# Wider products in a causal convolution and in LayerNorm's sums of a hybrid encoder trunk

## The reference, cut to what matters

```python
def conv_module(h, buf, w_pw1, b_pw1, w_dw, b_dw, ln_g, ln_b, w_pw2, b_pw2):
    u = h @ w_pw1 + b_pw1
    a, gt = jnp.split(u, 2, axis=-1)
    glu = a * jax.nn.sigmoid(gt)
    xp = jnp.concatenate([buf.astype(glu.dtype), glu], axis=1)
    y = causal_dwconv(xp, w_dw, b_dw)          # 31 taps, each channel by itself
    y = jax.nn.silu(layernorm(y, ln_g, ln_b))  # mean and variance over the 1024 channels
    return y @ w_pw2 + b_pw2, new_buf
...
def rmsnorm(x, g):
    y = xf * lax.rsqrt(jnp.mean(xf * xf, axis=-1, keepdims=True) + EPS)
```

## Time and profile before

| | us |
|---|---|
| median of 3 runs | 2890.53 (2886.12 to 2891.44) |
| profiled execution | 2888.88 |
| its span, first to last instruction | 2887.1 |
| mean granted clock of TensorE, as a share of full speed | 0.986 |

### The profile page before, as it was taken

How to read it: one execution, slowest core, us unless ns; L and a number is a source line. 1 busy time by engine, 2 the same in 40 slices (tenths; PEclk the granted TensorE clock), 3 DMA queues, 4 the chain that set the end, 5 groups by cost and what they waited for, 6 DMA issues and landing times.

```text
span 2887.1 us, 40334 instructions
## 1 busy us (share of the span) xinstructions
PE 2849.4 (99%) x16832; PEld 2798.9 (97%) x16832; DVE 1662.5 (58%) x1821; ACT 529.3 (18%) x647; POOL 834.4 (29%) x686
## 2 busy tenths in 40 slices
PE   8999999999999999999999999999999999999998
PEld 8999799999999999999999999989999999999998
DVE  8995336454545455466676667781744555454445
ACT  3001323111111111231111111121311111111122
POOL 5221154222222222243121222114322222222224
PEclk9999599999999999999999999999999999999999
DMA  5223021111111111121111110103111111111112
GB/s 152 57 59 57 0 109 44 38 43 44 44 38 41 44 44 40 41 108 52 46 45 38 45 46 31 47 30 116 38 43 44 44 39 41 44 44 39 41 45 79
DMA packets 109012, 147.07 MB, mean 51 GB/s; under 512 B 65265, under 2 KB 78065, under 8 KB 108913
## 3 DMA queue, kind: packets, MB, share of 16 engines
q1 hardware_dynamic: 48624, 112.48, 12.3%
q10 hardware_dynamic: 60288, 33.14, 4.0%
HBM read 129.13 MB, written 16.47 MB: 50 GB/s over the span
## 4 chain that ended last, share of the span: by engine, by line
PE 89%; DVE 9%; issue 1%; ACT 1%; POOL 0%; DMA 0%; DVEq 0%; ACTq 0%; POOLq 0%
PE BANKS L649 63%; PE BANKS L895 11%; PE BANKS L937 3%; PE BANKS L1123 3%; DVE BANKS L1678 1%; PE BANKS L722 1%; PE BANKS L720 1%; PE BANKS L857 1%; DVE HGA L2032 1%; DVE HGA L1997 1%; DVE HGA L2019 1%; PE BANKS L745 1%; DVE XL L1590 1%; PE BANKS L986 1%; DVE X L1678 1%
## 5 line engine op out<-in xcount | busy, mean ns | idle before, releaser
L535 POOL TENSOR_TENSOR SMALL<-WRAW 128x1 f32<-128x1 f32 x196 | 48.4, 247 | 1916.3 <-PE BANKS L649 1334.1
L649 PE MATMUL BANKS<-XH,WH 128*128 128x384 f32 x2592 | 592.0, 336 | 0.6 <-DVE X L1603 0.5
L649 PE MATMUL BANKS<-XL,WH 128*128 128x384 f32 x2592 | 588.6, 334 | 0.0
L649 PE MATMUL BANKS<-XH,WL 128*128 128x384 f32 x2592 | 588.6, 334 | 0.0
L538 POOL TENSOR_TENSOR WL<-WRAW,WH 128x1024 fp32r<-128x1024 f32 x196 | 476.5, 2431 | 15.7
L649 PEld LDWEIGHTS BANKS<-XL,WH 128*128 128x128 f32 x2592 | 462.2, 188 | 0.0
L649 PEld LDWEIGHTS BANKS<-XH,WL 128*128 128x128 f32 x2592 | 462.1, 188 | 0.0
L649 PEld LDWEIGHTS BANKS<-XH,WH 128*128 128x128 f32 x2592 | 460.4, 188 | 1.7 <-DVE X L1603 0.9
L1815 DVE TENSOR_TENSOR X<-BANKS,X 128x1152 f32<-128x1152 f32 x168 | 228.0, 1357 | 267.4 <-PE BANKS L649 206.4
L1872 DVE SCALAR_TENSOR_TENSOR ARENA<-ARENA 128x1168 f32<-128x1168 f32 x176 | 255.7, 1453 | 130.9 <-ACT ARENA L1377 122.2
L1377 ACT ACTIVATE ARENA<-ARENA 128x1168 f32<-128x1168 f32 x88 | 120.3, 1367 | 943.7 <-DVE ARENA L1612 943.7
(11 more groups left out here) (214 smaller groups left out, 3474.7 us busy)
## 6 DMA issues: line engine op xcount, KB each, us to landing
WRAW<-in_w SPq DMA_DIRECT2D x188, 512.0 KB, 3.5
X<-in_x SPq DMA_DIRECT2D x8, 576.0 KB, 9.0
X<-in_x ACTq DMA_DIRECT2D x8, 576.0 KB, 7.2
x_kept<-X ACTq DMA_DIRECT2D x8, 576.0 KB, 2.8
X<-x_kept ACTq DMA_DIRECT2D x8, 576.0 KB, 7.4
HGA<-taps_padded ACTq DMA_DIRECT2D x32, 128.0 KB, 3.5
HGA<-in_state ACTq DMA_DIRECT2D x8, 512.0 KB, 4.3
out_hgs<-HGA ACTq DMA_DIRECT2D x8, 512.0 KB, 2.6
```

The source lines that it names most:

```text
L535: nc.gpsimd.tensor_tensor(PAD, one, one, ALU.mult)
L649: ins = nc.tensor.matmul(ps_bank(n, c), w, x[:, third(c)], start=(k == 0 and q == 0), stop=(k == last and q == 2), skip_group_check=betwee ...
```

## The change

- `convolved`: each product takes the same 40 columns three times over (120 columns, by a dimension of stride 0), and twice or once where the bank ends (the eleventh and the twelfth group of a full bank). The extra results fall where the next groups write later, each with `start=True`.
- Twelve products of `mean` instead of seven stand ahead of the convolution of c = 7, and nine among its groups.
- `variance` and `fin_sum` multiply with 128 columns of ones in place of one. ScalarE reads every 128th column of the result.
- `idle_products` are added, 256 columns each, two records each: six and two around the last three `mean` products, and two, one and three around `spread_norm(1)` and `spread_norm(2)`. TensorE's wait for a free slot stands ahead of the first of the latter.
- GpSimd's splits of the first two weight units of the next product wait until VectorE has transposed the last channel's data.

```diff
+            pool.wait_ge(xt_rdy, len(TOEPLITZ))
             split(U_PW2)
             split(U_PW2 + 1)
...
-                    out = PS[:, n % 2 * NCH + g // BANK_GROUPS, at:at + COLS]
-                    nc.tensor.matmul(out, WT[:, g, 0, :], XT[0][:, :, g], start=True, stop=False,
-                                     skip_group_check=True)
-                    ins = nc.tensor.matmul(out, WT[:, g, 1, :], XT[1][:, :, g], start=False, stop=True,
-                                           skip_group_check=True)
+                    times = min(3, (512 - at) // COLS)
+                    out = PS[:, n % 2 * NCH + g // BANK_GROUPS, at:at + times * COLS].rearrange(
+                        "p (r b) -> p r b", r=times)
+                    for t in range(2):
+                        blocks_of = XT[t][:, :, g].rearrange("p (r b) -> p r b", r=1).broadcast_to([P, times, COLS])
+                        ins = nc.tensor.matmul(out, WT[:, g, t, :], blocks_of, start=t == 0, stop=t == 1,
+                                               skip_group_check=True)
...
-            ahead = len(parts) - (BLK // 2 - 2)
+            ahead = 12
...
+            def idle_products(times, out):
+                for _ in range(times):
+                    nc.tensor.matmul(out[:, 0:2 * P], IDENT, CONST[:, 0:2 * P], start=True, stop=True)
+            idle_products(6, MB[:, 0, :])
             for c in range(NCH):
                 mean(KD - 1, c)
+            idle_products(2, MB[:, 0, :])
...
-                        ins = nc.tensor.matmul(ps_bank(T_VAR, c)[:, t:t + 1],
-                                               LSQ[:, KD * c + 2 * p, t * P:(t + 1) * P], ONES[:, 0:1],
+                        ins = nc.tensor.matmul(ps_bank(T_VAR, c)[:, t * P:(t + 1) * P],
+                                               LSQ[:, KD * c + 2 * p, t * P:(t + 1) * P], ONES,
...
             variance(2)
+            free_slot(T_PW2)
+            idle_products(2, ps_bank(T_PW2, 2))
             spread_norm(1)
+            idle_products(1, ps_bank(T_PW2, 2))
             spread_norm(2)
+            idle_products(3, ps_bank(T_PW2, 2))
             pe.wait_ge(w_split, U_PW2 + 2)
-            free_slot(T_PW2)
...
-                        ins = nc.tensor.matmul(MB[:, c % 2, t:t + 1], squares[:, a:a + P], ONES[:, 0:1],
+                        ins = nc.tensor.matmul(MB[:, c % 2, t * P:(t + 1) * P], squares[:, a:a + P], ONES,
```

More of the change, by code:

```diff
@@ L1333, in ln_root @@
                 act.wait_ge(var_full, c + 1)
-                A(R9[:, c * NCH:(c + 1) * NCH], ps_bank(T_VAR, c)[:, 0:NCH], ACT.Sqrt, bias=EPSC, scale=1.0 / D
+                A(R9[:, c * NCH:(c + 1) * NCH], ps_bank(T_VAR, c)[:, 0:CW:P], ACT.Sqrt, bias=EPSC, scale=1.0 / D
                   ).then_inc(root_rdy, 1)
@@ L1552, in _ @@
                 act.wait_ge(fin_sums, c + 1)
-                A(R9[:, c * NCH:(c + 1) * NCH], MB[:, c % 2, 0:NCH], ACT.Sqrt, bias=EPSC, scale=1.0 / D
+                A(R9[:, c * NCH:(c + 1) * NCH], MB[:, c % 2, 0:CW:P], ACT.Sqrt, bias=EPSC, scale=1.0 / D
                   ).then_inc(fin_root, 1)
```

## The result

The changed kernel's median is 2915.31 us (2915.23 to 2916.34, 4 runs) against 2890.8 for the kernel before. The ratio is 1.0087, with a 95% interval of 1.0071 to 1.0103. The forecast was 2902.5, slower, with 2861 to 2914 as its range: the sign was right, the forecast change of 12.0 us was half of the measured one, and the time lies 1.3 us above the range. The profiled execution took 2915.35 us, 26.5 more than that of before.

A forecast was written before the change was run, and what follows sets the result against it. The prediction took PE's own work as the bound: busy 99% of the span, 89% of the chain. Its terms summed to +12.0 us on the profiled 2888.88, so 2900.9, median 2902.5, range 2861 to 2914.

The forecast's parts named there:

- 1, 2: four channels, and the fall of the clock at 250 us: Channels between value tiles: 120-column records at 0.180 us add 30.7 us; no clock fall at 250 us saves 1.5.
- 3: the last channel: The last channel's mean products and convolution: 35.6 us at full clock in place of 50.65, so -15.1 us.
- 4: later splits: GpSimd's splits of the next weight units, moved behind VectorE's transposes: needed 60 us later, so 0.
- 5: six idle products: Six idle products after the last convolution: 2.6 us of work in a 2.6 us wait, +0.2 us (0 to +1).
- 6: mean product to centring: First mean product to VectorE's start: 0.81 us at full clock in place of 1.69, so -0.9 us.
- 7: spreading to the dense products: From `spread_norm(0)` to the first dense product: faster sums, three idle products give back 1.3 us; -1.0 us (-1.9 to +3).
- 8: the tail: `fin_sum(2)` and the spreading behind it, at about half clock before: -0.4 us (-1 to 0).
- The upper bound: A 120-column convolution record takes at most 0.200 us, by the half clock's rate of 1.65 ns per column.
- The rival of free columns: Convolution records of 120 columns keep 0.112 us: sum -26.3 us, median 2864; chance 0.36.
- The rival in between: Convolution records of 120 columns take 0.145 to 0.160 us: sum -8 to 0, median 2882 to 2891; chance 0.08.
- The falling clock: Clock falls despite width, slowing dense products and mean records: +19 to +25 us, median 2909 to 2916; 0.11 with late idle products.

The follow-up runs named there:

- pair120: The changed kernel with `XT` in pairs, the columns of two neighbouring groups alternating: 2861.23 us, ratio 0.9886 to the kernel before.
- trial of distances: The changed kernel with extra unread products at its end: 120 columns took 0.112 us a record two elements apart, 0.156 at three, 0.212 at four, 0.208 at 32.
- cols40: The changed kernel with the convolution's 40 columns taken once, all its other edits kept: 2866.25 us (2863.11 to 2874.88, 6 runs).
- pair120_sums1: pair120 with one column in both LayerNorm's and the last norm's sums, as before the change: 2865.82 us.

## Why the prediction was right in sign and wrong in size

Point by point, by the steps of the prediction:

| step | forecast us | measured us |
|---|---|---|
| 1, 2: four channels, and the fall of the clock at 250 us | +30.7 - 1.5 | +40.8 |
| 3: the last channel | -15.1 | -12.0 |
| 4: later splits | 0 | 0.0 (taken out of pair120) |
| 5: six idle products | +0.2 | 0.0 |
| 6: mean product to centring | -0.9 | -0.7 |
| 7: spreading to the dense products | -1.0 | -1.3 |
| 8: the tail | -0.4 | -0.3 |
| sum | +12.0 | +26.5 |

The step that failed is one number: "So I take 1.5 ns per column: 120 columns take 0.180 us". The price is 0.207, and 80 columns take two thirds of it, about 0.138 (four of them start within 0.4 us). Four channels then cost 4 x (112 x 0.095 + 8 x 0.026) = 43.4 us, 12.7 more than forecast; 1.1 more than forecast came back. Of these 0.6 can be TensorE's waits (0.63 us of 198 before, none after); the rest isn't traced. The last channel came out 3.1 above its forecast. 12.7 - 1.1 + 3.1 = 14.7 of the 14.5 us missed; the rest are tenths in steps 5 to 8.

The mechanism, a limit on the rate of reads, was read rightly off the 228 ns of the earlier trace rows, and the trial of distances bears it out; what was misread is the slope. I divided the whole excess over one column, 59 ns, by the 39 further columns. The least durations for 40, 80 and 120 columns are 228 ns, 299 and 365 ns: the first 40 cost 59, the next 40 cost 71, the last 40 cost 66. It is as if a few columns came for nothing at the start of a record and the rest cost 1.7 ns each. In a stream every column has that price, 0.207 us / 120 = 1.72 ns. The upper bound failed the same way: it was set at the half clock's 1.65 ns because there the excess seemed gone. But a read price of 1.72 ns beside the array's own 1.65 would make only 3 ns over 39 columns, too little to see, and no run shows that the price of reads is the same at both clocks. So that row could not bound the price at full clock. With 0.207 us for 120 columns and 0.138 for 80 the sum had been +28.

The rival of free columns had 0.36 and is out for this layout; its sum, 2864, is within 3 us of pair120, where its condition holds (2861.23). The rival in between, 0.145 to 0.160 us because reads run ahead while the weights load, is out by the same 0.207. The falling clock did not come: the clock stayed full among the last channel's groups, at 0.207 us a record. Term 7 had its disturbance, the clock fell for part of it (0.81 over the stretch), and still came out 0.3 us better than taken. What it had wrong is the price of the three idle products, 1.3 us: taken out of pair120 they change nothing, since they stand where TensorE waits for VectorE.

## What to carry to other kernels

Look at how far apart the columns of a moving operand lie before widening it: in these runs, at full clock, float32 columns up to 8 bytes apart cost no more than side by side and from 16 bytes on twice as much (1.72 ns against 0.83), and products of 40 columns hid that, since their records start 0.112 us apart either way. When a cost is hidden, take its slope from two sizes where it shows, not from one size and zero. And a layout with pairs may serve both the engine that writes and the one that reads, as it did here. Before paying for a higher clock, look for a wait ahead of the stretch: in the one trace of cols40 the last channel kept its clock with 40 columns and no wait, where 40 columns behind a wait had lost it.

## What the runs showed of the hardware

- VectorE's block transposes of 128x1024 float32 take 1225 ns when they write two elements side by side, as when they write 32, and 2188 ns when each element goes 160 bytes on.
- Sums with one column let the clock of TensorE fall to 1.2 GHz where the same sums with 128 columns kept it at 2.4 through the first two thirds (pair120_sums1 against pair120). Behind the 2.84 us for which TensorE then waits for VectorE's diagonal, it fell with 128 columns too (0.57 from 320.4 to 323.6 us in pair120). At full clock the wide sums cost no more: six records start within 0.6 us with 1 column and with 128. The gain was 4.6 us.
- Records of 40 columns among dense products lost the clock for 3.2 us in the profiled run before and for 17 us in that of cols40; no other run with them has a trace. The times of cols40 spread by 12 us; the five kernels with 120 columns in pairs and everything else in its new place or nearly so spread by 0.6 to 5.9.
